# Three modulation groups moved from the projections into the attention of their layer

## Reference, cut to what matters

```
    for i in range(DEPTH):
        last = i == DEPTH - 1
        mod_x = (c_act @ ada_w[i] + ada_b[i]).reshape(bsz, 6, 1, D_MODEL)
        mod_c = (cc_act @ ada_w[i] + ada_b[i]).reshape(6, 1, 1, D_MODEL)

        hx = modulate(rms_norm(x, mix_norm_g[i]), mod_x[:, 0], mod_x[:, 1])
        hc = modulate(rms_norm(ctx, mix_norm_g[i]), mod_c[0], mod_c[1])
...
        o_a = window_attention(qa_x, ka_x, va_x, ka_c, va_c, a_sink[i])
        o_b = conv_module(ub_x, b_conv_w[i], b_conv_b[i], b_ln_g[i], b_ln_b[i])
        o_c = mla_blocks(qn_x, qr_x, jnp.concatenate([kn_x, kn_c], axis=1),
                         jnp.concatenate([kr_x, kr_c], axis=1),
                         jnp.concatenate([vc_x, vc_c], axis=1))
        x = x + mod_x[:, 2] * (jnp.concatenate([o_a, o_b, o_c], axis=-1) @ w_out[i])
...
        x = x + mod_x[:, 5] * ffn(modulate(rms_norm(x, ffn_norm_g[i]), mod_x[:, 3], mod_x[:, 4]))
```

## Time and profile before

| | |
|---|---|
| time, median of 3 executions | 1774.49 us (1768.44 to 1776.2) |
| profiled execution, first to last instruction (the one time that its page gives) | 1772.8 us |
| PE busy | 1656.5 us, 93% |
| DVE, ACT, POOL busy | 448.1, 309.7, 43.0 us |
| transfers | 394.76 MB, mean 223 GB/s |
| PE matmuls | 7998 |

### The profile page before, as it was taken

The page is one execution under the profiler, slowest core; times in us unless marked ns, Lnnn a source line. Parts: engine busy times, 40 slices in busy tenths (PEclk is TensorE's granted clock), DMA queues, the critical chain, the costliest instruction groups (busy, mean ns, idle before and its releaser), DMA issues.

```text
span 1772.8 us, 21037 instructions
## 1 busy us (share of the span) xinstructions
PE 1656.5 (93%) x7998; PEld 937.7 (53%) x7999; DVE 448.1 (25%) x1098; ACT 309.7 (17%) x721; POOL 43.0 (2%) x49
## 2 busy tenths in 40 slices
PE   3999879999999999999998999899989989999988
PEld 1454445444444444445665765685536555865464
DVE  1367794210000000003588330100201101001011
ACT  3135453210000000002345221000101010000110
POOL 1001000100000000000010100000000000000000
PEclk9999999999999999999999989999999999999999
DMA  9530610252141122115304269987799999977997
GB/s 379 223 143 0 246 41 25 89 223 91 71 166 71 71 73 93 71 71 231 125 11 180 73 255 422 390 291 278 292 420 421 422 422 422 377 269 290 422 421 324
DMA packets 56605, 394.76 MB, mean 223 GB/s; under 512 B 6480, under 2 KB 7888, under 8 KB 8912
## 3 DMA queue, kind: packets, MB, share of 16 engines
q1 hardware_dynamic: 56384, 393.63, 56.1%
q10 hardware_dynamic: 144, 0.01, 0.0%
HBM read 392.57 MB, written 1.05 MB: 222 GB/s over the span
## 4 chain that ended last, share of the span: by engine, by line
PE 79%; DMA 10%; DVE 7%; issue 2%; ACT 1%; SPq 1%; DVEq 0%; ACTq 0%
PE ps L688 17%; DMA ring<-in_stream 10%; PE ps L764 10%; PE ps L470 9%; PE ps L773 9%; PE ps L708 9%; PE ps L668 5%; PE ps L812 4%; PE ps L809 3%; PE ps L416 2%; PE ps L867 1%; PE ps L592 1%; PE ps L745 1%; PE ps L796 1%; DVE arena L1358 1%
## 5 line engine op out<-in xcount | busy, mean ns | idle before, releaser
L688 PE MATMUL ps<-hT,ring 128*128 128x512 f32 x704 | 302.7, 592 | 0.0
L764 PE MATMUL ps<-ring,arena 128*64 128x256 f32 x1056 | 243.2, 384 | 20.9 <-DMA ring<-in_stream 14.3
L767 PE MATMUL ps<-ring,arena 128*64 128x256 f32 x1056 | 243.7, 384 | 0.0
L688 PEld LDWEIGHTS ps<-hT,ring 128*128 128x128 f32 x704 | 133.5, 190 | 167.3 <-issue 166.4
L764 PEld LDWEIGHTS ps<-ring,arena 128*64 128x64 f32 x1056 | 139.9, 137 | 92.7 <-issue 33.6
L470 PE MATMUL ps<-hT,ring 128*128 128x512 f32 (+2 forms) x480 | 172.5, 515 | 2.4 <-ACT hT L921 2.2
L773 PE MATMUL ps<-ring,arena 128*128 128x256 f32 x704 | 155.6, 379 | 0.0
L708 PE MATMUL ps<-arena,ring 128*128 128x512 f32 x352 | 151.2, 592 | 0.0
L773 PEld LDWEIGHTS ps<-ring,arena 128*128 128x128 f32 x704 | 132.2, 190 | 17.1
L767 PEld LDWEIGHTS ps<-ring,arena 128*64 128x64 f32 x1056 | 140.0, 137 | 0.0
L470 PEld LDWEIGHTS ps<-hT,ring 128*128 128x128 f32 (+1 forms) x480 | 87.9, 185 | 81.7 <-issue 73.7
(11 more groups left out here) (188 smaller groups left out, 1345.7 us busy)
## 6 DMA issues: line engine op xcount, KB each, us to landing
ring<-in_stream SPq DMA_DIRECT2D x371, 1024.0 KB, 13.1
xT<-in_x SPq DMA_DIRECT2D x8, 256.0 KB, 4.2
cst<-in_consts SPq DMA_DIRECT2D x1, 1092.0 KB, 23.8
out_x<-xT SPq DMA_DIRECT2D x4, 256.0 KB, 2.6
par<-in_params SPq DMA_DIRECT2D x2, 75.0 KB, 2.3
cst<-in_consts SPq DMA_DIRECT2D x1, 128.5 KB, 2.2
moep<-in_moe SPq DMA_DIRECT2D x1, 36.0 KB, 25.5
ccol<-in_c ACTq DMA_DIRECT2D x1, 8.0 KB, 2.4
```

Of the source, the lines that this page charges most:

```text
L688: last = pe.matmul(ps[:, 2 * m + f % 2, :], ring[:, slot, m * 1024 + k * P:m * 1024 + (k + 1) * P], hT[:, k, :], start=(k == 0), stop=(k = ...
L764: a = pe.matmul(ps[0:64, b, 0:256], hTe[:, k, 0:64], ring[:, s1, k * 256:(k + 1) * 256], start=(k == 0), stop=(k == KD - 1))
L767: last = pe.matmul(ps[64:P, b, 0:256], hTe[:, k, 0:64], ring[:, s3, k * 256:(k + 1) * 256], start=(k == 0), stop=(k == KD - 1))
```

## The change

(0,2) leaves the projections for the place behind the first two score steps of layer 0's attention, where (0,4) was. (0,3) and (0,4) are cut into four pieces each of two k (8 matmuls), put between scores and turn of units 12 to 15 and 18 to 21; their `ada_turn` and `ada_store` follow in steps 16 and 22. (1,4) is cut into two pieces of four k (16 matmuls) at units 8 and 9 of layer 1, its turn in step 10. The units in the stream are ordered alike. The late groups use the two halves of bank 7 for rows and turned rows, since the values of the attention use bank 6. `ada_rows` of every group now also waits for `ada_mod` of the group before.

```
-ADA_AFTER_TILE = {(0, 7): (0, 2), (0, 23): (0, 3), (1, 23): (1, 4)}
-ADA_IN_ATTENTION = {0: [(0, 4)]}
+ADA_FIRST = {0: (0, 2)}
+ADA_PARTS = {0: [((0, 3), 12, 4), ((0, 4), 18, 4)], 1: [((1, 4), 8, 2)]}
+ADA_LATE = [key for parts in ADA_PARTS.values() for key, _, _ in parts]
...
+        def ada_at_banks(layer, g):
+
+            if (layer, g) in ADA_LATE:
+                return ps[:, 7, 0:256], ps[:, 7, 256:512]
+            return ps[:, 6, 0:256], ps[:, 7, 0:256]
...
-            def ada_rows(layer, g):
+            def ada_rows(layer, g, k0=0, k1=KD):
 
 
                 n = ada_at[layer, g]
-                slots = [arrived(("ada", layer, 4 * g + j)) for j in range(4)]
-                if n > 1:
-                    pe.wait_ge(ada_row, n - 1)
-                for k in range(KD):
+                if k0 == 0:
                     for j in range(4):
-                        last = pe.matmul(ps[32 * j:32 * j + 32, ADA_BANK, 0:256], cact[:, k, :],
-                                         ring[:, slots[j], k * 256:(k + 1) * 256], start=(k == 0), stop=(k == KD - 1))
+                        arrived(("ada", layer, 4 * g + j))
+                    if n > 1:
+                        pe.wait_ge(ada_row, n - 1)
+                        pe.wait_ge(ada_mod, n - 1)
+                    if (layer, g) in ADA_LATE:
+                        pe.wait_ge(z_done, 2 * layer + 1)
+                rows, _ = ada_at_banks(layer, g)
+                for k in range(k0, k1):
+                    for j in range(4):
+                        slot = UNIT_AT["ada", layer, 4 * g + j] % RING
+                        last = pe.matmul(rows[32 * j:32 * j + 32, :], cact[:, k, :],
+                                         ring[:, slot, k * 256:(k + 1) * 256], start=(k == 0), stop=(k == KD - 1))
                         first(last)
-                last.then_inc(ada_mm, 1)
-                owed[0] += 4
+                if k1 == KD:
+                    last.then_inc(ada_mm, 1)
+                    owed[0] += 4
...
-                    if (layer, t) in ADA_AFTER_TILE:
-                        ada_rows(*ADA_AFTER_TILE[layer, t])
-                    if (layer, t - 1) in ADA_AFTER_TILE:
-                        ada_turn(*ADA_AFTER_TILE[layer, t - 1])
-                if (layer, len(TILES) - 1) in ADA_AFTER_TILE:
-                    ada_turn(*ADA_AFTER_TILE[layer, len(TILES) - 1])
                 rotate(layer, len(TILES) - 3)
...
                     if a + 2 < len(units):
                         scores(layer, a + 2)
+                    for key, a0, count in ADA_PARTS[layer]:
+                        if a0 <= a < a0 + count:
+                            ada_rows(*key, (a - a0) * KD // count, (a - a0 + 1) * KD // count)
                     turn_probs(layer, a)
-                    for key in ADA_IN_ATTENTION.get(layer, []) if a == 0 else []:
-                        ada_turn(*key)
-                    if a == mean_at:
-                        for key in ADA_IN_ATTENTION.get(layer, []):
-                            pe.wait_ge(ada_mod, ada_at[key])
+                    if a == 0 and layer in ADA_FIRST:
+                        ada_turn(*ADA_FIRST[layer])
+                    for key, a0, count in ADA_PARTS[layer]:
+                        if a == a0 + count:
+                            ada_turn(*key)
+                    if a == mean_at and layer in ADA_FIRST:
+                        pe.wait_ge(ada_mod, ada_at[ADA_FIRST[layer]])
                     if a >= 1:
                         values(layer, a - 1)
```

More of the change, by code:

```diff
@@ L93, in mixer @@
             plan.append(("in", layer, u))
-            ada([ADA_AFTER_TILE[key] for key in ((layer, 2 * u + 1),) if key in ADA_AFTER_TILE])
-        ada([ADA_AFTER_TILE[key] for key in ((layer, len(TILES) - 1),) if key in ADA_AFTER_TILE])
-        ada(ADA_IN_ATTENTION.get(layer, []))
+        ada([ADA_FIRST[x] for x in (layer,) if x in ADA_FIRST])
+        ada([key for key, _, _ in ADA_PARTS[layer]])
         plan.extend(("out", layer, u) for u in range(OUT_U))
@@ L427, in ada_turn @@
                 for half in range(2):
-                    last = pe.transpose(ps[:, ADAT_BANK, half * P:(half + 1) * P],
+                    last = pe.transpose(ada_at_banks(layer, g)[1][:, half * P:(half + 1) * P],
                                         adarow[:, half * P:(half + 1) * P], c_("ident"))
@@ L622, in attention @@
                 pe.wait_ge(spread_done, 2 * (layer + 1))
-                pe.wait_ge(ada_mod, ada_at[ADA_AFTER_TILE[layer, len(TILES) - 1]])
+                if layer:
+                    pe.wait_ge(ada_mod, ada_at[1, 3])
                 scores(layer, 0)
                 scores(layer, 1)
-                for key in ADA_IN_ATTENTION.get(layer, []):
-                    ada_rows(*key)
+                if layer in ADA_FIRST:
+                    ada_rows(*ADA_FIRST[layer])
                 mean_at, var_at = CONV_AT[layer]
@@ L928, in ada_copy @@
                     act.wait_ge(ada_tr, n - 1)
-                act.activation(adarow[:, :], ps[:, ADA_BANK, 0:256], ACT.Copy).then_inc(ada_row, 1)
+                act.activation(adarow[:, :], ada_at_banks(layer, g)[0], ACT.Copy).then_inc(ada_row, 1)
             def tile_squares(layer, t):
@@ L978, in projections @@
                         group_root(layer, t - 1)
-                    if (layer, t - 1) in ADA_AFTER_TILE:
-                        ada_copy(*ADA_AFTER_TILE[layer, t - 1])
-                if (layer, len(TILES) - 1) in ADA_AFTER_TILE:
-                    ada_copy(*ADA_AFTER_TILE[layer, len(TILES) - 1])
             def softmax(layer, a):
@@ L1021, in attention @@
                 softmax(layer, 1)
-                for key in ADA_IN_ATTENTION.get(layer, []):
-                    ada_copy(*key)
+                if layer in ADA_FIRST:
+                    ada_copy(*ADA_FIRST[layer])
                 for a in range(len(units)):
@@ L1033, in attention @@
                         conv_norm(layer)
+                    for key, a0, count in ADA_PARTS[layer]:
+                        if a == a0 + count - 1:
+                            ada_copy(*key)
                 act.preload_act_table(ACT.Sigmoid)
@@ L1179, in ada_store @@
                 dve.wait_ge(ada_tr, n)
-                rows = ps[:, ADAT_BANK, 0:256].rearrange("p (h j s) -> p h j s", h=2, j=4)
+                rows = ada_at_banks(layer, g)[1].rearrange("p (h j s) -> p h j s", h=2, j=4)
                 b = p_(layer, "ada_b", KD * g, KD).rearrange("p (j h) -> p h j", h=2)
@@ L1386, in attention @@
                     turned(layer, a)
-                    for key in ADA_IN_ATTENTION.get(layer, []) if a == 0 else []:
-                        ada_store(*key)
+                    if a == 0 and layer in ADA_FIRST:
+                        ada_store(*ADA_FIRST[layer])
+                    for key, a0, count in ADA_PARTS[layer]:
+                        if a == a0 + count:
+                            ada_store(*key)
                     if a + 1 < len(units):
```

6 lines of the change are left out of this document (1 added, 5 removed).

## The result

The changed kernel takes 1787.99 us (1786.74 to 1791.37, 6 runs), the kernel before beside it 1775.35 (1768.44 to 1780.82): ratio 1.0070, 95% interval 1.0055 to 1.0085. It is 12.6 us slower; +3.1 was forecast, and the time lies above the range. The profiled executions differ by 14.0 us in span.

What follows compares the result with a forecast made beforehand. PE was taken to bound layer 0's mid-projections, with DVE taking turns at their end and PE having hardly any room in attention part C. Terms -4.8, -1.3, -2.1, +2.8, +6.0, +2.5 gave +3.1 us: 1777.5 us, range 1771.5 to 1783.

Steps and rivals of the forecast that it cites:

- Term 1: Middle of layer 0's projections: taking (0,2)'s rows and turn out of PE's queue saves 4.8 us.
- Term 2: End of layer 0's projections: without (0,3) the last rotation waits only for DVE's rotary instruction, saving 1.3 us.
- Term 3: End of layer 1's projections: without (1,4) after the last tile, DVE's next instruction comes earlier, saving 2.1 us.
- Term 4: Behind norms 1 and 2: the new wait for `ada_mod` delays the second rows by 1.4 us each, +2.8 us.
- Term 5: Layer 0's attention: eight pieces and two turns, less the PE waits that cover them, +6.0 us (2.5 to 7.5).
- The low stretch ahead of it: Layer 0, around the last rotation: half clock after a new 3.1 us PE gap, 1 to 3 us, one chance in two.
- Term 6: Layer 1's attention: (1,4)'s two pieces and turn against a 1.42 us wait at unit 9, +2.5 us (1 to 4).
- Cost nothing: Experts' start: loading their first four units after layer 1's attention, not at its start, adds 0 us.
- rival C: Experts: four units loaded later make the stream late, 11.2 us plus 3.1, 1788.8 us; chance 0.02 (0.06 with a low-clock version).

Runs made afterwards that it cites:

- e6: Changed kernel without the new wait for `ada_mod` ahead of rows, except for the three late groups; 1780.75 us, ratio 1.0024 to the kernel before.
- e9: Changed kernel with (0,2) after layer 0's last projection tile and (0,3) behind the first two score steps, so no pieces at units 12 to 15; 1782.14 us.
- e10: Changed kernel with four tiny matmuls just ahead of the loop over the experts; 1777.15 us, ratio 1.0010 to the kernel before.
- e7: Changed kernel with (1,4)'s two pieces at units 9 and 10 of layer 1, not 8 and 9; 1784.15 us, ratio 1.0047 to the kernel before.
- e16: e12 with (1,4) late, in two pieces at units 9 and 10 of layer 1; 1763.51 us, ratio 0.9944 to the kernel before.
- e5: Changed kernel with four tiny matmuls at the head, ahead of the first square sum; 1776.46 us, ratio 1.0005 to the kernel before.
- e13: Kernel before with three tiny matmuls just ahead of the loop over the experts; 1768.07 us, ratio 0.9975.
- e15: Changed kernel with eight tiny matmuls just ahead of the loop over the experts; 1783.48 us, ratio 1.0052 to the kernel before.
- e18: Changed kernel with (1,4) whole behind the first two score steps of layer 1's attention; 1780.23 us, ratio 1.0038 to the kernel before.
- e12: Kernel before with (0,2) ending layer 0's projections, (0,3) and (1,4) behind first score steps, (0,4) whole at unit 11, four tiny matmuls at the loop; 1763.16 us.

## Why the prediction was wrong

**Term 1, -4.8: right.** The last but one rotation comes at 188.53; less the 0.58 by which the bursts stand later already at 90.82, that is -4.91. **Term 2, -1.3: right**, -1.26 more at 192.31. **Term 3, -2.1: right**, 106.7 to 104.6 us from projection to rotation. DVE's end of the rotary step set terms 2 and 3, PE's own queue term 1, as worked out.

**Term 4, +2.8: the waits right, what followed not.** They measured 1.43 and 1.51 at the places named. But the clock fell behind the first, 1.7 us more (e6; not in e9). I had looked at the clock where gaps of 3 us arise, not where a short wait comes on top of others.

**Term 5, +6.0: right.** From unit 11's turn (243.07, 3.92 earlier than in the earlier trace rows) to the output projection (289.95, 2.19 later than 287.76) it is 6.1. The low stretch ahead of it I had put at one in two and left out of the sum. It came (e9): from the last rotation to unit 11's turn the changed kernel takes 1.67 us more than before, 0.9 in e10.

**Term 6, +2.5: failed.** It set rows and turn "against a wait of 1.42 at unit 9" and named no other wait. The rows of the first piece have one of their own, for `z_done`, which I had in the diff and did not date: 1.61 us, and 4.2 in all. Without it the pieces cost 1.3 (e7).

**The clean sum ahead of the experts** is e10 against before: 1009.0 - 1001.6 = +7.4, where I had 3.1. The 4.3 between are 0.9 of clock in layer 0, 1.8 behind norm 1, 0.2 behind norm 2 and 1.7 of term 6, less 0.3 of small rests. The changed kernel's own profiled execution takes 10.0 us more from first projection to experts; the other 2.6 are low stretches that in e10 are shorter or lie ahead of the first projection (153.0 against 151.3 us, 97.6 against 96.8). Its first projection began 1.1 us earlier than in the kernel before, which leaves the 8.9.

**The step that failed most is "Cost nothing" for the experts.** I saw only their loads, and rival C was a stream that comes late. The loads came in time: waits for them fell by 7 us, and e16 shows that late slots cost nothing. What grew were waits for "issue", to all appearance for PE's instructions, +12.5 us of them. 5.1 us reached the end: other waits shrank by nearly as much, those of all PE rows for the stream alone from 17.1 to 8.4 us, since the ring fills while PE stands, and the matmuls took 4.7 us more at the lower clock. That the measured 1787.99 lies next to rival C's 1788.8 is chance. I had not read the "issue" waits in the experts of the kernel before at all, 18.1 us with five waits, and so never asked what hangs on them. Four tiny matmuls at the loop take 10.8 us off the changed kernel and 7.7 off the kernel before; with them in both, the change costs 10.1 (1777.15 - 1767.03), of which 7.4 is the sum above and 2.7 is left in the experts.

Open stays by what rule these waits fall. That they are PE's code being loaded rests on the transfers of instructions in them and on their answer to shifts of three to eight matmuls; that the longer experts of the changed kernel are their doing, on e5 and e10, where four matmuls take 8.0 and 9.0 us off the experts and the waits fall from 30.6 to 11.5 and 10.2. The loop's start alone does not decide (4450: two waits in e13, eight in the changed kernel and e7), and with one profiled execution a kernel I can't say how often each occurs.

## What to carry to other kernels

Before costing an edit, read the "issue" waits of loops with branches that the edit doesn't touch: they can answer to a few instructions more or less ahead of them, by as much as the edit itself, so time a change also with a shift of its code. For each moved step, date every semaphore that its first instruction waits for, not just the engines at its side. Put filler work in a wait that is longer than it is: whole at unit 11 a group cost nothing net, in eight small pieces over busy units two groups cost 6 us.

## What the runs showed of the hardware

- Waits of PE for "issue" in the loop last 2.7 to 5.2 us in the kernels before and after, while the weight stream keeps the DMA engines full (100.7% in the rows above); over all kernels 1.1 (e15) to 7.9 (e18). In all 13 of the two kernels a transfer of 16 KB on the instruction queue starts within the wait.
- A wait of 1.43 us, behind one of 0.50, was enough for the granted clock to fall to 0.57 in the next 4 us, in eight of nine kernels; in e9 the same two waits left it at 1.00. That behind norm 2, of 1.51, cost 1.57 in all and no clock. The Trainium skill, "TensorE: Matmul & The Clock Gate", "Why this matters for your kernels", warns of idle gaps between bursts; the trace agrees for 3.10 us, and shows that shorter ones can do it. A wait of 2.30 us ahead of the last rotation of layer 1 was followed by no drop at 936.39 of the changed kernel and by one at 922.76 of e12.
- 128 tiny matmuls of 128x8 at the head of the program brought PE's first projection 33.9 us later, 0.26 us each.
